# A decoder block on one core: the down projections' moving operand taken as two interleaved runs of columns

## The reference

```python
proj = jnp.einsum('bsd,de->bse', x, w_in[l])          # q, k, v, conv B, C, h, two gates
merged = sigmoid(g_conv) * short_conv(...) + sigmoid(g_attn) * sliding_window_attention(...)
x = layer_norm(ALPHA * x + einsum('bse,ed->bsd', merged, w_out[l]), ln1_g[l], ln1_b[l])
hid = jax.nn.silu(jnp.einsum('bsd,df->bsf', x, w_gate[l])) * jnp.einsum('bsd,df->bsf', x, w_up[l])
ffn = jnp.einsum('bsf,fd->bsd', hid, w_down[l])       # D_FF = 2816
x = layer_norm(ALPHA * x + ffn, ln2_g[l], ln2_b[l])
```

## Time and profile before

| | us |
|---|---|
| median of 3 runs | 1458.66 |
| lowest, highest | 1458.49, 1458.88 |
| the profiled execution, its time | 1459.72 |
| its span, from the first to the last instruction | 1457.9 |
| TensorE busy in the span | 1438.5 |
| VectorE busy | 796.0 |
| GpSimd busy | 601.2 |
| ScalarE busy | 485.2 |

### The profile page before, as it was taken

One profiled execution on the slowest core, in us unless ns is written; L12 is line 12 of the kernel. 1 busy time (PEld: TensorE's weight loads), 2 busy tenths in 40 slices (PEclk: granted clock), 3 DMA queues, 4 the chain that ended last, 5 costly groups with the idle time before them and its releaser, 6 DMA issues. The chain is left out here.

```text
span 1457.9 us, 19033 instructions
## 1 busy us (share of the span) xinstructions
PE 1438.5 (99%) x6658; PEld 1195.1 (82%) x6658; DVE 796.0 (55%) x1196; ACT 485.2 (33%) x933; POOL 601.2 (41%) x374
## 2 busy tenths in 40 slices
PE   9999999999999999999999899999999999999997
PEld 7888888888888888887887688888888888888886
DVE  3126564557457644766866835545345353454547
ACT  4433433343334323334255332312323223232133
POOL 2221122212312231214873484655637547364464
PEclk9999999999999999999999999999999999999999
DMA  6211111111111011011420121212111112112112
GB/s 174 59 44 44 44 29 58 41 31 43 43 43 43 29 51 50 29 43 58 124 79 15 58 73 37 65 43 65 50 44 58 50 58 64 29 60 61 45 51 116
DMA packets 128407, 80.22 MB, mean 55 GB/s; under 512 B 8433, under 2 KB 123121, under 8 KB 128369
## 3 DMA queue, kind: packets, MB, share of 16 engines
q1 hardware_dynamic: 128368, 79.73, 18.2%
HBM read 75.53 MB, written 4.19 MB: 55 GB/s over the span
## 5 line engine op out<-in xcount | busy, mean ns | idle before, releaser
L1341 PE MATMUL ps<-act_hi,w_hi 128*128 128x512 f32 x864 | 339.3, 393 | 1.1 <-DVE act_lo L906 1.1
L476 POOL TENSOR_TENSOR w_lo<-raw,w_hi 128x1024 fp32r<-128x1024 f32 x54 | 131.6, 2437 | 505.3 <-ACT w_hi L616 505.3
L1342 PE MATMUL ps<-act_lo,w_hi 128*128 128x512 f32 x864 | 337.3, 390 | 0.0
L1343 PE MATMUL ps<-act_hi,w_lo 128*128 128x512 f32 x864 | 337.1, 390 | 0.0
L564 POOL TENSOR_TENSOR w_lo<-raw,w_hi 128x512 fp32r<-128x512 f32 x80 | 108.3, 1354 | 227.8 <-ACT w_hi L819 227.8
L1343 PEld LDWEIGHTS ps<-act_hi,w_lo 128*128 128x128 f32 x864 | 162.6, 188 | 34.5
L1341 PEld LDWEIGHTS ps<-act_hi,w_hi 128*128 128x128 f32 x864 | 162.6, 188 | 33.5 <-issue 1.3
L1342 PEld LDWEIGHTS ps<-act_lo,w_hi 128*128 128x128 f32 x864 | 162.8, 188 | 32.1
L1341 PE MATMUL ps<-hid_hi,wd_hi 128*128 128x512 f32 x320 | 125.0, 391 | 4.2 <-DVE res L1184 4.2
L1190 DVE TENSOR_TENSOR res<-res,ps 128x512 f32<-128x512 f32 x128 | 87.9, 687 | 68.3 <-PE ps L1343 67.8
L1343 PE MATMUL ps<-hid_hi,wd_lo 128*128 128x512 f32 x320 | 124.6, 389 | 0.0
(11 more groups left out here) (193 smaller groups left out, 2547.5 us busy)
## 6 DMA issues: line engine op xcount, KB each, us to landing
raw<-in_w_in SPq DMA_DIRECT2D x52, 512.0 KB, 3.8
raw_d<-in_w_down SPq DMA_DIRECT2D x22, 512.0 KB, 3.2
raw<-in_w_gate SPq DMA_DIRECT2D x40, 256.0 KB, 2.8
raw<-in_w_up SPq DMA_DIRECT2D x40, 256.0 KB, 3.1
raw<-in_w_out SPq DMA_DIRECT2D x16, 512.0 KB, 3.6
xs<-in_x SPq DMA_DIRECT2D x8, 512.0 KB, 8.0
out<-rows SPq DMA_DIRECT2D x7, 512.0 KB, 2.6
raw_b<-in_w_gate SPq DMA_DIRECT2D x1, 512.0 KB, 5.1
```

Of the source, the lines that this page charges most:

```text
L476: pool.tensor_tensor(w_lo[:, slot], raw[:, slot], fp(w_hi[:, slot]), ALU.subtract).then_inc(w_lo_s, 1)
L1341: pe.matmul(bank, w_h(t), a_hi(t), start=(t == 0), stop=False)
L1342: pe.matmul(bank, w_h(t), a_lo(t), start=False, stop=False)
L1343: last = pe.matmul(bank, w_l(t), a_hi(t), start=False, stop=(t == tiles - 1))
```

## The change

Two things, which belong together. In `down` the moving operand of each matmul, 512 columns of `hid_hi` or `hid_lo`, is handed over through an access pattern that goes through columns 0, 256, 1, 257, 2, 258 and so on. The matmul still writes its 512 results one beside the other, so column 2b + a of the bank now holds token 256a + b of the half. In `add_down` VectorE reads the bank as two runs of 256 columns in steps of two, which puts the tokens back in order, and views `res` as two runs of 256 neighbouring columns. Numbers of instructions, of columns and all waits are the same; every engine's instructions stand in the same order. The weights, the pair products, the gate and up products and the last rows are not touched.

```diff
             def add_down(i, c, v, how):
                 h, m = v // DT, v % DT
-                tile = res[:, m, half(h)]
+                tile = res[:, m, half(h)].rearrange("p (a b) -> p a b", a=2)
+                bank = ps[:, 4 + v % 4, :].rearrange("p (b a) -> p a b", a=2)
                 dve.wait_ge(d_s, i * 32 + (16 * c + v + 1))
                 if how == "first":
-                    dve.scalar_tensor_tensor(out=tile, in0=tile, scalar=ALPHA, in1=ps[:, 4 + v % 4, :], op0=ALU.mult,
+                    dve.scalar_tensor_tensor(out=tile, in0=tile, scalar=ALPHA, in1=bank, op0=ALU.mult,
                                              op1=ALU.add).then_inc(add_s, 1)
...
                 else:
-                    dve.tensor_tensor(tile, tile, ps[:, 4 + v % 4, :], ALU.add).then_inc(add_s, 1)
+                    dve.tensor_tensor(tile, tile, bank, ALU.add).then_inc(add_s, 1)
...
+            def folded(ap):
+
+                return ap.rearrange("p (a b) -> p b a", a=2)
+
             def down(i, c, h, m):
...
                 product(ps[:, 4 + v % 4, :], lambda t: wd_hi[:, t, blk(m)], lambda t: wd_lo[:, t, blk(m)],
-                        lambda t: hid_hi[:, t, half(h)], lambda t: hid_lo[:, t, half(h)], 2).then_inc(d_s, 1)
+                        lambda t: folded(hid_hi[:, t, half(h)]), lambda t: folded(hid_lo[:, t, half(h)]),
+                        2).then_inc(d_s, 1)
```

More of the change, by code:

```diff
@@ L1180, in add_down @@
                 h, m = v // DT, v % DT
-                tile = res[:, m, half(h)]
+                tile = res[:, m, half(h)].rearrange("p (a b) -> p a b", a=2)
+                bank = ps[:, 4 + v % 4, :].rearrange("p (b a) -> p a b", a=2)
                 dve.wait_ge(d_s, i * 32 + (16 * c + v + 1))
                 if how == "first":
-                    dve.scalar_tensor_tensor(out=tile, in0=tile, scalar=ALPHA, in1=ps[:, 4 + v % 4, :], op0=ALU.mult,
+                    dve.scalar_tensor_tensor(out=tile, in0=tile, scalar=ALPHA, in1=bank, op0=ALU.mult,
                                              op1=ALU.add).then_inc(add_s, 1)
                 elif how == "biased":
-                    dve.scalar_tensor_tensor(out=tile, in0=tile, scalar=alpha_b[:, m:m + 1], in1=ps[:, 4 + v % 4, :],
+                    dve.scalar_tensor_tensor(out=tile, in0=tile, scalar=alpha_b[:, m:m + 1], in1=bank,
                                              op0=ALU.add, op1=ALU.add).then_inc(add_s, 1)
                 else:
-                    dve.tensor_tensor(tile, tile, ps[:, 4 + v % 4, :], ALU.add).then_inc(add_s, 1)
+                    dve.tensor_tensor(tile, tile, bank, ALU.add).then_inc(add_s, 1)
             dve.tensor_scalar(alpha_b[:], lnb[:], ALPHA, None, ALU.mult).then_inc(ab_s, 1)
```

## The result

The changed kernel takes 1449.11 us (median of 4 runs, 1449.08 to 1450.62), the kernel before 1458.77 us (4 runs, 1458.49 to 1459.08). The ratio is 0.9936, 95% interval 0.9924 to 0.9947: **faster by 0.64%**, 9.7 us. The forecast was 1658 us, with a range from 1457 to 1675; the sign was wrong, and the time lies outside. The profiled execution of after took 1449.08 us, 10.64 less than that of before (1459.72).

What follows compares the result with a forecast made beforehand. TensorE's matmul stream was taken to bound the kernel. Profiled 1459.72 us, plus 204.8 for the slower moving read, less 5.5 of hidden waits, adds 0, gave 1659.0; as a median 1658 us, range 1457 to 1675.

Steps and rivals of the forecast that it cites:

- the sign: Whole kernel: slower than before by more than 0.2%, chance 0.80; faster had 0.02.
- What bounds the kernel: Whole kernel: TensorE's matmul stream sets the end; any change to the down products' 226.7 ns lands there unchanged.
- What the 226.7 ns are made of: Down matmuls: 213.3 ns at one column a cycle plus 13.4 ns each, where alone a faster read can win.
- the far end below nothing: Down products, lower bound: all of the 13.4 ns a matmul goes, 12.9 us in all.
- The price of the folded read: TensorE's moving operand in down: one column in two cycles, 440.0 ns a matmul, +204.8 us.
- The rule that was weighed: SBUF reads by 16-byte lines: two hits hide one access, so one hit costs two column times, +204.8 us.
- The waits that a longer stream hides: First down stretch: 5.51 us of TensorE waits for VectorE's adds all vanish, -5.5 us.
- The adds: VectorE's 160 adds reading the bank in steps of two: either bound fits beside TensorE's stream, 0 us.
- rival 2: TensorE unchanged but VectorE's adds slower: 1462 us, or 1471 us at 1466 ns an add; chance 0.04.
- the rival that had it fall: Clock lowered as the array takes a column only every other cycle: clock alone 17 us after ten stretches, 1662 or 1675 us.
- Rival 5: Down matmuls faster: the 13.4 ns each vanish, 1446 us; chance 0.02.

Runs made afterwards that it cites:

- `orders`: Each of the 16 units of a down stretch takes its moving columns in an order of its own, adds plain; 1519.78 us in one run.
- `steps_of_four`: Changed kernel with the moving operand of all down products in steps of four columns (16 bytes), adds plain; 1677.84 us in one run.
- `adds_only`: Changed kernel with the moving operand back in plain order, only VectorE's adds keeping steps of two; 1458.76 us, ratio to before 1.0001.
- `fixed_cost`: Each of the 16 units of a down stretch gets its own column order, moving width or number of weight columns; 1451.92 us in one run.

## Why the prediction was wrong, point by point

- **What bounds the kernel: right.** TensorE's stream sets the end, the down products are 960 matmuls at 226.7 ns, and what their distance changed by arrived at the end: 960 x 10.9 ns = 10.5 us, less 0.55 of longer waits in the first stretch, is 9.9 us, beside 9.66 between the medians.
- **What the 226.7 ns are made of: right, and the key was in it.** The sum named 13.4 ns above one column a cycle as all that a faster read could win. 10.9 of them were won. The prediction put the price of losing all of it, 12.9 us, at "the far end below nothing", wrote that "No row excludes it, and none speaks for it", and gave it 2 in 100. The point to take is that it should have asked why a plain stream pays 13.4 ns a matmul at all, since that is a cost of the very read that the change alters. A cost without a known cause at the place of a change is a reason for a wide chance on both sides. The earlier trace rows held a hint that was passed over: at half the clock the same plain stream has no surplus (426.7 ns, 512 / 1.2), so it is not a fixed time that every matmul pays. Nothing here tested that further.
- **The price of the folded read, "one column in two cycles": wrong, the step that failed.** This term of the sum was +213.3 ns a matmul, +204.8 us in all; measured are -10.9 ns and -10.5 us. It rested on the sentence that "no read that fetches neighbours together can serve two columns in a row". The runs show that serving two in a *row* is not what counts. `orders` has the same two runs in turns of one at 215.8 ns and in turns of two at 328.3 ns, and steps of two, where neighbours share a group of four columns, at 453.7. ScalarE's 1.03 ns a column, which was to be the nearest row, said nothing of TensorE. Why the folded order is not only free but faster stays open: theory L tells it, but it is inferred from times and misses units 8 to 11 of `orders`.
- **The rule that was weighed.** The Trainium skill, Advanced Engine Details and Errata (SBUF Cachelines), wants two hits in a row on a line of 16 bytes. By that rule unit 6 (steps of 8 bytes, two hits a line) should be free and the folded order (one hit, then the other line) should pay. Measured: 453.7 and 215.8 ns, the reverse of both. The size that I read out of it, a doubling, is right where a line does serve one column only: 460 ns in `steps_of_four`. Counted for every second column of the stream apart the rule fits better, with four hits better than two, though not for units 8 to 11.
- **The waits that a longer stream hides, -5.5 us: right, shown by `steps_of_four`,** whose first stretch has none of them left. Its time is the sum of before on the same chip, the longer stream and these waits: 1459.59 + 960 x (0.4598 - 0.2267) - 5.5 = 1677.9 us, and 1677.84 was measured. With the shorter stream of the change the same waits grew by 0.55 us.
- **The adds: right.** 686 ns, free; `adds_only` has ratio 1.0001. One reading in rival 2 is off without harm: the wait that six adds stand ahead of is the last long one (1.19 us), not the longest, which is 1.68 us and belongs to the seventh unit, behind three adds.
- **The clock: no fall,** neither in the change nor in the slow stream; the rival that had it fall is out.
- **Rival 5 was the one that happened,** at 1446 us where 1449.1 was measured: 2.5 of the 13.4 ns stay (2.4 us), and the first stretch's waits took half a microsecond. It was listed without a mechanism, so that it stands there is no merit of the reasoning.

## What to carry to other kernels

Where TensorE is the bound and streams fp32r operands of 512 columns, hand it the moving operand as two runs in turns of one column, and let the readers of the bank step by two: 226.7 becomes 215.8 ns a matmul, 5%, at no cost to the readers, and 52 us over this whole kernel. Steps of 2, 4 and 16 columns take about twice as long as plain, and so do eight runs; no other order tried that passes each column once was faster than plain. Only fp32r operands were measured. And when a stream costs more than its columns, measure orders of it: sixteen of them fit into one run, one in each unit of a loop that comes again.

## What the runs showed of the hardware that was not expected

- A plain fp32r stream is not the fastest: 226.7 ns for 512 columns, and 228 to 236 when it begins at column 1, 4, 8, 16 or 128 of the tile; as two runs in turns of one it is 215.4 to 216.5 from each start tried, for distances of 4, 16, 64, 256, 257 and 1024 columns. Even one column repeated is 215.7.
- Steps of 2 and of 4 columns cost the same, 454 and 461 ns; four runs in turn 283, six 297, eight 487. That columns at even and odd places are fetched apart is the theory that fits best of those tried, and it told the times of units 9, 10, 11, 13, 14 and 15 of `fixed_cost` ahead, to within 5 ns; it is inferred from times, not seen, has no number for lanes with several open groups, and gives 227 where turns of 4 to 64 columns take 251 to 232.
- The surplus of a plain stream is there with 2 weight columns as with 128 (230.5 and 226.7 ns); what sets its size is open. Weight columns in steps of 8 lengthen the load from 0.19 to 0.33 us, and plain and folded then take 243.5 and 240.5 ns, most likely at the load's pace.
